# A two-layer trunk in one launch: half of the first four tiles' features loaded and multiplied ahead at each layer end, and modulation slices and prefetches moved

## The reference, cut to what matters

```python
def modulate(x, g, shift, scale):
    return rmsnorm(x, g) * (1.0 + scale) + shift
...
    o_lat = jnp.concatenate([diff_out(o_a), o_b], axis=-1)
...
def diff_out(o):
    return (rmsnorm(o, subln_g) * (1.0 - lam_init)).reshape(B, N, DIFF_HEADS * DIFF_V)
...
def sq_relu_mlp(h, w1, w2):
    return jnp.square(jax.nn.relu(h @ w1)) @ w2
```

## Time and profile before

| | us |
|---|---|
| median of three runs | 3868.09 |
| lowest, highest | 3865.18, 3874.36 |
| the profiled execution | 3870.9 |
| its span in the profile | 3868.8 |

### The profile page before, as it was taken

One profiled execution on the slowest core, in us unless ns is written; L12 is line 12 of the kernel. 1 busy time (PEld: TensorE's weight loads), 2 busy tenths in 40 slices (PEclk: granted clock), 3 DMA queues, 4 the chain that ended last, 5 costly groups with the idle time before them and its releaser, 6 DMA issues. The chain is left out here.

```text
span 3868.8 us, 48121 instructions
## 1 busy us (share of the span) xinstructions
PE 3549.2 (92%) x17792; PEld 2894.3 (75%) x17792; DVE 2154.3 (56%) x3141; ACT 1335.7 (35%) x2411; POOL 172.5 (4%) x178
## 2 busy tenths in 40 slices
PE   6888888897899999999998979799899899999999
PEld 3677666786788888888876868577688678888887
DVE  4768755786663444444455446588688463333333
ACT  3433334564431111111115545466466341111111
POOL 1100010000120000000001100000000020000000
PEclk8899899998999999999998989799899899999999
DMA  5546674422321222121214354442344311111112
GB/s 185 176 143 230 182 156 88 114 62 89 91 80 56 69 63 70 56 59 57 69 44 150 136 164 136 111 106 63 61 103 93 115 52 44 49 49 51 50 54 66
DMA packets 431973, 366.51 MB, mean 95 GB/s; under 512 B 104246, under 2 KB 374982, under 8 KB 426694
## 3 DMA queue, kind: packets, MB, share of 16 engines
q1 hardware_dynamic: 431813, 364.42, 33.3%
HBM read 276.67 MB, written 87.69 MB: 94 GB/s over the span
## 5 line engine op out<-in xcount | busy, mean ns | idle before, releaser
L2256 DVE SCALAR_TENSOR_TENSOR xT<-ps,mods,xT 128x1024 f32<-128x1024 f32 x192 | 189.4, 1014 | 425.4 <-PE ps L2470 425.4
L2470 PE MATMUL ps<-e_gh,e_w2h 128*128 128x512 f32 x1280 | 357.5, 377 | 5.9 <-DVE e_w2l L2715 3.6
L2765 DVE TENSOR_TENSOR e_plain<-e_plain 128x1280 f32<-128x1280 f32 (+1 forms) x64 | 87.0, 1359 | 481.9 <-ACT e_plain L2630 481.9
L2470 PE MATMUL ps<-e_gl,e_w2h 128*128 128x512 f32 x1280 | 353.5, 374 | 0.0
L2470 PE MATMUL ps<-e_gh,e_w2l 128*128 128x512 f32 x1280 | 353.1, 374 | 0.0
L2630 ACT ACTIVATE e_plain<-ps 128x1280 f32<-128x1280 f32 (+1 forms) x64 | 72.7, 1136 | 761.5 <-PE ps L2470 757.5
L2470 PE MATMUL ps<-e_hh,e_w1h 128*128 128x512 f32 (+1 forms) x1200 | 327.6, 371 | 0.0
L2470 PE MATMUL ps<-e_hh,e_w1l 128*128 128x512 f32 (+1 forms) x1200 | 327.5, 371 | 0.0
L2470 PE MATMUL ps<-e_hl,e_w1h 128*128 128x512 f32 (+1 forms) x1200 | 327.5, 371 | 0.0
L2470 PEld LDWEIGHTS ps<-e_gh,e_w2h 128*128 128x128 f32 x1280 | 225.4, 191 | 55.3 <-DVE e_gl L2769 8.0
L2470 PEld LDWEIGHTS ps<-e_gh,e_w2l 128*128 128x128 f32 x1280 | 226.8, 191 | 43.5
(11 more groups left out here) (397 smaller groups left out, 7631.7 us busy)
## 6 DMA issues: line engine op xcount, KB each, us to landing
e_raw<-in_mlp_w SPq DMA_DIRECT2D x64, 512.0 KB, 4.2
e_raw<-in_mlp_w SPq DMA_DIRECT2D x128, 256.0 KB, 3.0
rstd<-in_ada_w SPq DMA_DIRECT2D x64, 384.0 KB, 3.4
e_raw<-in_w_out SPq DMA_DIRECT2D x40, 512.0 KB, 4.0
qkC<-pc_stage SPq DMA_DIRECT2D x72, 192.0 KB, 2.9
hT<-pb_hb SPq DMA_DIRECT2D x10, 1024.0 KB, 5.6
pa_hb<-hT SPq DMA_DIRECT2D x10, 1024.0 KB, 6.7
qkA<-pa_stage SPq DMA_DIRECT2D x20, 512.0 KB, 3.5
```

Of the source, the lines that this page charges most:

```text
L2256: ins = k.nc.vector.scalar_tensor_tensor(out=x, in0=ps, scalar=k.mods[:, layer, gate, bass.ds(n, 1), w], in1=x, op0=ALU.mult, op1=ALU.add)
L2470: mm = pe.matmul(k.ps[:, SB * (e % 2) + b, 0:n], w[:, e % 2, f], m[:, f, c0:c0 + n], start=(f == 0 and x == 0), stop=(f == nf - 1 and x == 2))
L2765: nc.vector.tensor_tensor(g, g, g, ALU.mult).then_inc(s.sqg, 1)
```

## The change

Four things are changed.

1. **Rows ahead.** A new object `RowsAhead` loads, while the last attention phase of a layer still runs, the half of the first four tiles' features that the phase before had finished (1 MB in one transfer): features 512 to 1023 for e0, 0 to 511 for e1. At the layer end PE turns these first, ACT and DVE split them, and PE does the 12 products of units 0 and 1 that need only them; then come the other halves and the other 12 products of each unit. The first four row loads are halved, and the weights of units 0 and 1 are issued earlier.
2. **Slices.** In pb four slices stand behind each value unit (the third) of tiles 1 to 8, and none behind the head units; the sums follow two jobs after a group's last slice. pa keeps its two slices a job.
3. **Loads moved.** `ahead_of.load` goes from the end of the first pair to the start of the last one, in ab and in ac.
4. ad loads its `RowsAhead` at the start of its last pair, aa after the third head.

```diff
+class RowsAhead:
+        self.rows = k.nc.alloc_sbuf_tensor_at(f"{name}_rows", [P, 4, KT // 2 * P], F32, offset=self.offset)
...
+    def load(self, sp):
+        rows = self.k.mix[self.layer].rearrange("(t p) d -> p t d", p=P)
+        sp.dma_start(self.rows[:], rows[:, 0:4, self.first * P:(self.first + KT // 2) * P]).then_inc(self.loaded, 16)
...
+    SUMS = 2 if keeps_h else 3
...
     def slices_at(n):
-        g, y = (n - FIRST) // PERIOD, (n - FIRST) % PERIOD
-        if n < FIRST or g >= NG:
+        if not NG:
             return range(0)
-        busy = PERIOD - 2 * (2 - ACCS)
-        return range(g * KT + min(KT, y * KT // busy), g * KT + min(KT, (y + 1) * KT // busy))
+        t, j = jobs[n]
+        if keeps_h:
+            return range(4 * (t - 1), 4 * t) if j == U - 1 and 0 < t <= NG * KT // 4 else range(0)
+        return range(2 * (n - U), 2 * (n - U) + 2) if U <= n < U + NG * KT // 2 else range(0)
...
+                    if last and ahead_of is not None:
+                        ahead_of.load(sp)
+                    if last and rows_of is not None:
+                        rows_of.load(sp)
...
-                    if first and ahead_of is not None:
-                        ahead_of.load(sp)
...
+                        elif p == 0:
+                            rows_of.load(sp)
...
                 fetch_rows(0)
+                fetch_out(0)
                 fetch_rows(1)
                 if subln is not None:
                     sp.dma_start(gain[:], subln.unsqueeze(0).broadcast_to([P, P])).then_inc(s.g, 16)
-                fetch_out(0)
+                fetch_out(1)
                 fetch_rows(2)
                 fetch_rows(3)
-                fetch_out(1)
...
                 for t in tiles_of[0]:
+                    turn_early(t)
+                for u in range(2):
+                    out_unit(u, fs=early_f)
+                for t in tiles_of[0]:
                     turn(t)
                 for u in range(NU):
-                    out_unit(u)
+                    if u < 2:
+                        out_unit(u, begun=True, fs=late_f)
+                    else:
+                        out_unit(u)
...
+                for t in tiles_of[0]:
+                    high_early(t)
                 cut_out(0)
                 if subln is not None:
                     roots(0)
+                cut_out(1)
...
+                for t in tiles_of[0]:
+                    low_early(t)
                 cut_out(0)
                 for t in tiles_of[0]:
                     if subln is not None:
                         norm(t)
+                    if t == 0:
+                        cut_out(1)
                     if t:
                         low_rows(t - 1)
```

More of the change, by code:

```diff
@@ L673, in _ @@
                         turn(m)
-                    for g in group_after(n, 3) if NG else ():
+                    for g in group_after(n, SUMS):
                         vector_sums(g)
@@ L677, in _ @@
                     turn(m)
-                for n in range(N, N + 3):
-                    for g in group_after(n, 3) if NG else ():
+                for n in range(N, N + SUMS):
+                    for g in group_after(n, SUMS):
                         vector_sums(g)
@@ L883, in _ @@
                     low_part(before)
-                for n in range(N, N + 4):
-                    for g in group_after(n, 4) if NG else ():
+                for n in range(N, N + SUMS + 1):
+                    for g in group_after(n, SUMS + 1):
                         vector_sum(g)
@@ L1438, in steps_of_head, with attend @@
     return out, blocks
-def attend(k, name, pieces, heads, load_head, parts, split, v_width, mix, mix_col, sink=None, bias=None, beside=None, ahead=None, ahead_of=None):
+def attend(k, name, pieces, heads, load_head, parts, split, v_width, mix, mix_col, sink=None, bias=None, beside=None, ahead=None, ahead_of=None, rows_of=None):
     nc = k.nc
@@ L1544, in attend @@
             assert other is None or nc.sbuf_base <= other.end
+        assert rows_of is None or nc.sbuf_base <= rows_of.offset and rows_of.offset + 8192 <= ahead.end
         def near_loaded(eng, i, p):
@@ L1989, in bias_loader, with attend_diff @@
     return load
-def attend_diff(k, name, ins, ahead):
+def attend_diff(k, name, ins, ahead, rows_of):
     nc = k.nc
@@ L2013, in attend_diff @@
         TB, OB = 6, 7
-        assert nc.sbuf_base <= ahead.end
+        assert nc.sbuf_base <= ahead.end and SBUF_END - 23 * 1024 <= rows_of.offset
         def scores(b):
@@ L2258, in add_gated, with layer_end @@
     return ins
-def layer_end(k, name, layer, n_tok, parts, w_out, w1, w2, subln=None, following=None):
+def layer_end(k, name, layer, n_tok, parts, w_out, w1, w2, ahead, subln=None, following=None):
     nc = k.nc
@@ L2275, in layer_end, with halves @@
     names = ("in0 in1 in2 in3 g sqa red root ri ya yb T hi lo wr0 wr1 whi wlo mm x tick sq acc sum std rec f fm hh h "
-             "relu sqg gh g2 aw aacc asum modd scaled T2 cp st sq2 acc2 sum2")
+             "relu sqg gh g2 aw aacc asum modd scaled T2 cp st sq2 acc2 sum2 TE hiE loE")
+    early_f = range(ahead.first, ahead.first + KT // 2)
+    late_f = [f for f in range(KT) if f not in early_f]
+    NE = len(tiles_of[0])
+    assert NE == 4
+    def halves(t):
+        return late_f if t < NE else range(KT)
     def sum_bank(p):
@@ L2306, in layer_end @@
         w2h, w2l = sb("w2h", [P, 2, F, P], F32R), sb("w2l", [P, 2, F, P], F32R)
+        assert ahead.offset == at + 8 * F * n_tok + 3 * 8 * KT * P
         stat = sb("stat", [P, 3, 512])
@@ L2356, in fetch_rows @@
                         sp.wait_ge(s.T, t - RB + 1)
-                    sp.dma_start(rows[:, t % RB], k.mix[layer][t * P:(t + 1) * P]).then_inc(rows_in[t % RB], 16)
+                    c = slice(halves(t)[0] * P, (halves(t)[-1] + 1) * P)
+                    sp.dma_start(rows[:, t % RB, c], k.mix[layer][t * P:(t + 1) * P, c]).then_inc(rows_in[t % RB], 16)
                 def fetch_out(u):
@@ L2546, in high_rows, with high_early @@
                 def high_rows(t):
+                    fs = slice(halves(t)[0], halves(t)[-1] + 1)
                     act.wait_ge(s.T, t + 1)
-                    nc.scalar.copy(hh[:, :, t * P:(t + 1) * P], turned(t)).then_inc(s.hi, 1)
+                    nc.scalar.copy(hh[:, fs, t * P:(t + 1) * P], turned(t)[:, fs]).then_inc(s.hi, 1)
+                def high_early(t):
+                    fs = slice(early_f[0], early_f[-1] + 1)
+                    act.wait_ge(s.TE, t + 1)
+                    nc.scalar.copy(hh[:, fs, t * P:(t + 1) * P], turned(t)[:, fs]).then_inc(s.hiE, 1)
                 def cut_out(u):
@@ L2675, in low_rows, with low_early @@
                     dve.wait_ge(s.hi, t + 1)
-                    q = slice(t * P, (t + 1) * P)
-                    nc.vector.tensor_tensor(hl[:, :, q], turned(t), f32(hh[:, :, q]), ALU.subtract).then_inc(s.lo, 1)
+                    fs, q = slice(halves(t)[0], halves(t)[-1] + 1), slice(t * P, (t + 1) * P)
+                    nc.vector.tensor_tensor(hl[:, fs, q], turned(t)[:, fs], f32(hh[:, fs, q]), ALU.subtract).then_inc(s.lo, 1)
+                def low_early(t):
+                    dve.wait_ge(s.hiE, t + 1)
+                    fs, q = slice(early_f[0], early_f[-1] + 1), slice(t * P, (t + 1) * P)
+                    nc.vector.tensor_tensor(hl[:, fs, q], turned(t)[:, fs], f32(hh[:, fs, q]), ALU.subtract).then_inc(s.loE, 1)
                 def cut_out(u):
@@ L2868, in trunk @@
                load_d,
-               "two", True, HD, k.mix[1], 512, bias=bias_loader(k), ahead=ahead_d)
-        layer_end(k, "e1", 1, SEQ, [(0, 512), (512, 512)], ins["w_out"][1], ins["mlp_w1"][1], ins["mlp_w2"][1])
+               "two", True, HD, k.mix[1], 512, bias=bias_loader(k), ahead=ahead_d, rows_of=rows_1)
+        layer_end(k, "e1", 1, SEQ, [(0, 512), (512, 512)], ins["w_out"][1], ins["mlp_w1"][1], ins["mlp_w2"][1], rows_1)
         k.phases.end()
```

62 lines of the change are left out of this document (41 added, 21 removed).

## The result

| | before | changed |
|---|---|---|
| median of 4 runs, us | 3866.64 | 3826.29 |
| lowest, highest | 3863.24, 3874.36 | 3825.24, 3833.54 |
| ratio of the medians, 95% interval | 1 | 0.9897, 0.9877 to 0.9917 |
| the profiled execution's span | 3868.8 | 3831.6 |

40.4 us less, where 39.5 were forecast. The profiled execution of the changed kernel is the slowest of its four, and its span is 37.2 us shorter than the span before.

What follows compares the result with a forecast made beforehand. PE, busy for 92% of the span, was taken as the bound, with the gains in its standstills. Gains of 22 (pb), 10.5 (ab), 3 (e0) and 4 (e1) sum to 39.5 us: median 3828.6, range 3822 to 3837.

Steps and rivals of the forecast that it cites:

- pb: New slice places remove PE's 16.4 us of waits and nearly 10 of low clock: 22 us less, bounds 14 and 26.
- the heads' low part is what comes next on DVE: In pb the heads' low part meets POOL's instruction, costs 2.1 us, and leaves PE waiting 0.5 in eight tiles, 4 us.
- The rule of the Trainium skill: Two-input DVE and GpSimd instructions on SBUF exclude each other, the second fully blocked; pb's gain would be 18, not 22.
- rival D: Slower: in pb each of eight slice instructions takes 1.27 us; at 21.5 us a tile the kernel takes 3871; chance 0.03.
- ab: Moving the load ends PE's 9.08 us wait for keys and the lower clock after it: 10.5 us less, bounds 5 and 11.
- rival C: Part of ab's wait stays, since the turned bias tables alone fill the queues; 5.5 us less gain, 3834.1; chance 0.08.
- e0: Early halves at this layer end, held back by the wait for the gain: 3 us less, bounds 0 and 5.5.
- e1: Early halves at this layer end, with no norm and no gain: 4 us less, bounds 1 and 5.5.
- the time of unit 2: In layer end e1 unit 2's weights land near 3046, are split at 3048, and it starts there instead of 3051.9.
- A: POOL decides in pb: PE waits 2 us or more per tile at lower clock; pb gives 10, total 3840.6; chance 0.16.
- B: The layer ends give nothing, losing the 7 us forecast there: 3835.6; chance 0.11.
- E: The change doesn't reach PE, slices stay bound to DVE's total work: pb gives 0, the rest 17.5, 3851; chance 0.04.

Runs made afterwards that it cites:

- e4: The changed kernel with DVE's low part of the heads moved behind the multiplication by the reciprocal; 3833.42 us, ratio 0.9906 to the kernel before.
- e2: The kernel before with only the loads for aa and ad moved to the start of the last pair; 3856.36 us, ratio 0.9963.
- e5: The changed kernel with SP issuing weights of units 2 and 3 ahead of rows of tiles 4 to 7, both layer ends; 3818.4 us, ratio 0.987 to before.
- e9: The changed kernel itself, unaltered, run again on another chip; 3823.41 us, ratio 0.9883 to the kernel before.
- e7: The changed kernel with the norms of tiles 2 and 3 in layer end e0 one place earlier; 3821.69 us, ratio 0.9875 to before.
- e6: The changed kernel with DVE's wait for the norm's gain behind the early low parts and first weight split; 3818.22 us, ratio 0.9869 to before.
- e1: As a run (in "D and E fell in e1"), not the layer end: the kernel before with only the slices' new places; 3842.76 us, ratio 0.9926.
- e8: The changed kernel with weights of units 2 and 3 first, gain's wait later and norms earlier; 3819.61 us, ratio 0.9875 to before.
- e10: The changed kernel with weights of units 2 and 3 first, gain later, norms earlier, run again with more rounds; 3818.26 us, ratio 0.9864 to before.

## Why the prediction was right, point by point

**The total** was right, 40.4 against 39.5 (a median of 3826.29 against 3828.6; the kernel before has one more run now, which moved its own median by 1.5). That it came so close is luck in part: pb gave 5.8 more than forecast and e1 4 less, and these two errors cancelled. The profiled executions, 37.2 apart, would have said some 2 less than forecast.

**pb: 27.8 instead of 22.** The ceiling was read rightly. From the first to the tenth turn of query heads it was 168.1 us before and is 141.7 now (113.78 to 255.50), 26.4 less, where I had 26 from the tile without a wait; most of the other 1.4 lies ahead of the first turn, in the start of pb, which varies from run to run. Waits and low clock went together. The step that failed is what I made of "the heads' low part is what comes next on DVE": that it would meet POOL I had right, but I charged the 2.1 us to it, and a residual wait of 0.5 in eight tiles. In the trace the low part starts 0.03 us after POOL and isn't held; the product behind it is, and PE doesn't need that for another unit. e4 put the low part behind POOL's start and brought such a wait about, in four tiles and not eight, since in tiles with sums PE comes later. That its 0.49 agrees with my 0.5 is luck: in e4 the low part was held 1.4 us, not 2.1, and began another 0.9 later than in the changed kernel. So the term should have been 26, with nothing taken off.

**The rule of the Trainium skill** (SBUF — State Buffer, Who interferes with whom) that I had set against the row fits the traces better than my 2.1 us as a fixed price. What is held ends with POOL's instruction: 142.63 + 1.97 = 144.60 against 144.44 in the changed kernel, 142.65 against 142.10 in e4. POOL is held, too: where the low part began with POOL, POOL took 2.96 us, and 2.39 where DVE's two-input instruction came later. By the recorded starts POOL was ahead by 0.03 us all the same, so starts this near don't tell from the profile who is first. What I lacked was who comes first. By that rule I had 18 for pb, because I let the low part come second. One sum is off beside: a tile of 21.5 us in rival D gives 3872, not 3871.

**ab: 10.3 instead of 10.5,** by the mechanism told; rival C fell in e2. **pa, ac, the row loads:** nothing, within what these stretches vary by.

**e0: 2.8 instead of 3.** The gain's wait ended 7.11 us into e0, by a hair beyond the 7 that I had named as proof against me; in the profiles of e5 and e9 it was 6.79 and 6.96, and 7.28 in e7, so the mark was drawn too close. The first product came 13.05 us after SP's first issue (13), the late halves at 30.3 (30.9), at the lower clock as I had it. The chain of waits is shown, and the clock was a lucky guess: with the same code in e0, e4 and e5 kept the higher level for most of the late halves and reached the fifth tile's turn 37.0 and 37.1 us in, which would have made the gain about 4.5. e6 confirms that the gain's wait took time from the change: 5.0 us, not the "some 3" that I named, since the whole late chain hangs on it.

**e1: 0 instead of 4.** The step that failed is the time of unit 2. I saw that its weights are issued behind the late turns and 2 MB of rows, and put their landing 25.4 us after SP's first issue; it was 27.2. The issue came 1.5 us later than I had it, because the early halves ended 16.2 us in and not 15.4, and the late turns with them. Unit 2 started 29.6 us in instead of 27.4, still 1.7 nearer than before (31.2). And I gave that wait of 1.99 no clock: PE fell to the lower level for three and a half us (mean granted clock 0.52), which took the 1.7. My bound of 1 us was too high; another 0.9 went behind PE's last instruction, to SP's clearing of semaphores, which I hadn't looked at. e5 shows the cause, as it makes the late landing and the wait disappear.

**The rivals.** A did not come in, for the reason above. Half of B came true, e1's; the half on e0 did not. D and E fell in e1.

## What to carry to other kernels

Work that is fed to an engine in slices can cost much or nothing by its place (27.7 us in pb here): put it behind the unit that no other engine waits for, then ask which instruction is now beside POOL's. When a phase's start is made faster, follow each transfer that the old start had hidden, since an issue that waits for a later step becomes the next bound; here two issues moved in SP's queue turned a part worth nothing into one of about 4 us, in three profiles of four. Compare stretches between the same two instructions rather than totals when a few us are at stake, and take the clock of each stretch with them.

## What the runs showed of the hardware

- DVE and POOL in pb: the two-input instruction on DVE that comes while POOL's runs is held until about POOL's end (0.28 became 1.97 in the changed kernel, 0.68 became 2.05 in e4). In e4 a reciprocal (0.17 us) and the multiplication with an input from PSUM (0.29 us) ran beside POOL's, no slower than elsewhere in pb. POOL is held by a two-input DVE instruction, too, that begins before it or with it: POOL's took 2.34 us with DVE idle (the first of the kernel before), 2.57 and 2.83 later in that kernel, where a slice instruction had 0.32 and 0.59 us left at POOL's start, and 2.96 in the changed kernel, where the low part began 0.03 us after it and took 0.68.
- Clearing semaphores in SP's queue at the program's end took some 0.06 us each, 0.42 once: 3.1 us for 57, 3.9 for 62.
- The same stop of 1.40 us before the same 24 products was followed by the higher level in e8 and by the lower one in e10, and cost 1.5 us there. In e0 the late halves took 8.5, 7.5, 7.0 and 7.0 us in the four profiles with that same code (changed, e9, e4, e5), behind the same stop.
- e0 behind the fifth tile's turn ran the same instructions in 1084.8 to 1090.4 us. PE's waits differ by 0.2 us only between the changed kernel and e4 (7.4 and 7.2 in all for the output matrix's weights), which took 1089.9 and 1084.8. The difference is clock in single stretches of 100 us: 511 products at 0.98 in the changed kernel, 518 at 1.00 in e4 (columns as in the earlier trace rows; the first line is the changed kernel's, the second e4's).

```profile
1220.00:1320.00 100.00, 99.55 (x511) 84.40 (x510) 44.50 (x51) 10.08 (x12) 0.00 (x0) 0.98 0.24 67
```

```profile
1225.00:1325.00 100.00, 99.56 (x518) 84.44 (x517) 44.16 (x50) 10.94 (x13) 0.00 (x0) 1.00 0.24 67
```
